# Remainders of three gate units formed by adding DMA transfers instead of subtractions on the vector engine

## The reference, cut to what matters

```python
h = rms_norm(x, attn_norm_g[l])
proj = jnp.matmul(h, w_in[l])            # 1024 x 4608
u_conv, q, k, v = ...                    # the first 2560 columns
gates = jax.nn.sigmoid(proj[..., o3:]).reshape(B, S, N_BRANCH, D)   # 2048 columns
conv_out = conformer_conv(u_conv, ...)   # depthwise, 31 taps, then layer norm and silu
...
merged = (gates[:, :, 0] * jnp.matmul(conv_out, w_conv_out[l])
          + gates[:, :, 1] * jnp.matmul(attn_out, w_attn_out[l]))
```

## Time and profile before

| | |
|---|---|
| median of 2 runs | 1041.17 us (1039.8 to 1042.54) |
| profiled execution | 1040.6 us, span 1038.8 us |
| busy: PE, DVE, ACT, POOL | 906.6, 458.1, 350.5, 8.0 us |
| mean granted TensorE clock | 0.941 |
| read from HBM | 298.84 MB, 289 GB/s over the span |

### The profile page before, as it was taken

The page is one execution under the profiler, slowest core; times in us unless marked ns, Lnnn a source line. Parts: engine busy times, 40 slices in busy tenths (PEclk is TensorE's granted clock), DMA queues, the critical chain, the costliest instruction groups (busy, mean ns, idle before and its releaser), DMA issues.

```text
span 1038.8 us, 14337 instructions
## 1 busy us (share of the span) xinstructions
PE 906.6 (87%) x6040; PEld 659.7 (64%) x6040; DVE 458.1 (44%) x804; ACT 350.5 (34%) x561; POOL 8.0 (1%) x14
## 2 busy tenths in 40 slices
PE   8999999999889947858775766999999989999997
PEld 7969878955246411313222131488999989999886
DVE  6899858511010010100101010188656676988752
ACT  5453483311010000100000010349565645756542
POOL 1000000000000000000000000000100000000000
PEclk9999999999999987978888896999999999999999
DMA  9866434989999999999999999982524245664451
GB/s 332 295 224 228 178 122 170 393 338 420 415 411 426 382 429 423 426 425 425 429 418 432 421 428 425 404 290 82 166 101 160 86 158 163 198 206 166 168 197 41
DMA packets 78493, 301.27 MB, mean 290 GB/s; under 512 B 4195, under 2 KB 30948, under 8 KB 62818
## 3 DMA queue, kind: packets, MB, share of 16 engines
q1 hardware_dynamic: 76640, 298.82, 73.0%
q10 hardware_dynamic: 1458, 1.07, 0.4%
q0 software_dynamic: 336, 0.53, 0.3%
HBM read 298.84 MB, written 1.05 MB: 289 GB/s over the span
## 4 chain that ended last, share of the span: by engine, by line
PE 59%; DMA 27%; DVE 8%; ACT 3%; issue 1%; SPq 1%; DVEq 0%; ACTq 0%
PE bank L1412 11%; DMA ring<-in_w_gate_e_dram 9%; DMA ring<-in_w_down_e_dram 8%; PE bank L1079 8%; DMA ring<-in_w_up_e_dram 7%; PE bank L1430 6%; PE bank L1303 3%; PE bank L1318 3%; PE bank L781 3%; PE bank L1137 3%; PE bank L688 2%; PE bank L715 2%; DVE big L1971 2%; DMA qvpr<-in_w_down_e_dram 2%; PE bank L1109 2%; PE bank L955 2%
## 5 line engine op out<-in xcount | busy, mean ns | idle before, releaser
L1079 PE MATMUL bank<-ring,big 128*32 128x512 f32 x768 | 163.9, 711 | 76.5 <-DMA ring<-in_w_up_e_dram 38.6
L1079 PEld LDWEIGHTS bank<-ring,big 128*32 128x32 f32 x768 | 38.8, 127 | 193.8 <-issue 90.1
L352 DVE TENSOR_TENSOR ring_parts<-ring,ring_parts 128x2048 fp32r<-128x2048 f32 (+1 forms) x54 | 118.8, 2248 | 35.9 <-ACT ring_parts L344 35.5
L344 ACT ACTIVATE ring_parts<-ring 128x2048 fp32r<-128x2048 f32 (+1 forms) x53 | 96.6, 1874 | 55.5 <-DMA ring<-in_w_up_dram 26.1
L2261 DVE TENSOR_TENSOR xT<-bank,xT 128x512 f32<-128x512 f32 x32 | 22.1, 692 | 137.0 <-PE bank L1123 137.0
L1412 PE MATMUL bank<-mrg_parts,ring_parts 128*128 128x256 f32 x640 | 82.3, 281 | 0.0
L1412 PEld LDWEIGHTS bank<-mrg_parts,ring_parts 128*128 128x128 f32 x640 | 78.5, 189 | 0.0
L2218 DVE TENSOR_TENSOR big<-big,const 128x128 f32<-128x128 f32 x14 | 3.5, 289 | 154.4 <-PE bank L1066 154.4
L1079 PE MATMUL bank<-hs,big 128*32 128x512 f32 x128 | 67.8, 683 | 0.0
L1109 PE MATMUL bank<-ring,big 128*32 128x512 f32 x336 | 45.8, 673 | 18.9 <-DMA ring<-in_w_down_e_dram 16.8
L1079 PE MATMUL bank<-qvpr,big 128*32 128x512 f32 x112 | 60.7, 696 | 0.6 <-DMA qvpr<-in_w_gate_e_dram 0.6
(11 more groups left out here) (423 smaller groups left out, 1627.3 us busy)
## 6 DMA issues: line engine op xcount, KB each, us to landing
ring<-in_w_up_e_dram SPq DMA_DIRECT2D x24, 2048.0 KB, 28.8
ring<-in_w_gate_e_dram SPq DMA_DIRECT2D x24, 2048.0 KB, 22.4
ring<-in_w_down_e_dram SPq DMA_DIRECT2D x17, 2048.0 KB, 21.5
ring<-in_w_in_dram SPq DMA_DIRECT2D x12, 2048.0 KB, 14.2
ring<-in_w_up_dram SPq DMA_DIRECT2D x22, 1024.0 KB, 7.2
ring<-in_w_down_e_dram SPq DMA_DIRECT2D x12, 1024.0 KB, 20.3
ring<-in_w_down_dram SPq DMA_DIRECT2D x5, 2048.0 KB, 7.9
ring<-in_w_out_dram SPq DMA_DIRECT2D x4, 2048.0 KB, 9.8
```

Source lines behind the costliest of these rows:

```text
L344: signal(act.activation(pairs[stage][u % 3][0][:, part], raws[stage][u % 3][:, part], ACT.Copy), stage + "_hi")
L352: signal(eng.tensor_tensor(lo[:, part], raws[stage][u % 3][:, part], hi[:, part].bitcast(F32), ALU.subtract), name)
L1079: mm = pe.matmul(bank[part][CAP * j:CAP * j + CAP, :], xeT[:, c, CAP * j:CAP * j + CAP], w[j][c], start=(c == 0), stop=(c == DC - 1))
```

## The change

For gate units 0, 1 and 2 the remainder is no longer formed by DVE. ACT writes the rounded weights with their sign turned (`scale=-1.0`) into `GATE_HI`, and then copies that, -hi, over the weights in their slot. GpSimd's queue then reads the same weights from HBM a second time with DMAs that add to what is in the slot (`accum_op=ALU.add`): -hi + W = lo. It issues two such DMAs of 1 MB for a unit, one for each half, and waits for both of a unit before it issues those of the next. PE multiplies (-hi) x h1_hi, (-hi) x h1_lo, and, now as the third product, lo x (-h1_hi), so that the whole sum has its sign turned; the sigmoid takes that back with `scale=-1.0`. The negated activations `h1_neg` are two further copies of 1024 columns on ACT. The semaphore `gate_hi` now counts four steps for a unit, `gate_lo` 16 for each DMA.

```diff
+        h1_neg = [parts["mrg"][:, T * k:][:, 0:T] for k in range(4)] + [parts["sq"][:, T * k:][:, 0:T] for k in range(4)]
...
             signal(pool.tensor_copy(pairs["in"][0][0][:, h:], raws["in"][0][:, h:]), "in_hi")
+            for u in range(3):
+                if u:
+                    pool.wait_ge(S["gate_lo"], 32 * u)
+                for i in range(2):
+                    pool.wait_ge(S["gate_hi"], 4 * u + 2 + i + 1)
+                    dst = ring_r[PLAIN_AT[1 + u]][:, 2048 * i:2048 * i + 2048].rearrange("p (k n) -> p k n", k=4)
+                    pool.dma_start(dst, w_plain[1 + u][:, 4 * i:4 * i + 4].bitcast(F32R), accum_op=ALU.add).then_inc(S["gate_lo"], 16)
...
-                            if m == 0 and k % 4 == 0 and which < 2:
-                                pe.wait_ge(S[("gate_hi", "gate_lo")[which]], 2 * u + k // 4 + 1)
-                            w = lo[:, k] if which == 1 else hi[k // 4][:, k % 4]
-                            x = h1_lo[:, k * T:k * T + T] if which == 2 else h1_hi[k]
+                            if m == 0 and k % 4 == 0 and which == 0:
+                                pe.wait_ge(S["gate_hi"], 4 * u + k // 4 + 1)
+                            if (m, which, k) == (0, 2, 0):
+                                pe.wait_ge(S["gate_lo"], 32 * (u + 1))
+                                pe.wait_ge(S["h1_hi"], 6)
+                            w = lo[:, k] if which == 2 else hi[k // 4][:, k % 4]
+                            x = (h1_hi[k], h1_lo[:, k * T:k * T + T], h1_neg[k])[which]
...
-                move(("gt", m), big[:, m * T:m * T + T], T, ACT.Sigmoid)
+                move(("gt", m), big[:, m * T:m * T + T], T, ACT.Sigmoid, scale=-1.0 if m < 12 else 1.0)
...
                 for i in range(2):
-                    signal(act.activation(GATE_HI[u][i], ring[PLAIN_AT[1 + u]][:, 2048 * i:2048 * i + 2048], ACT.Copy), "gate_hi")
+                    signal(act.activation(GATE_HI[u][i], ring[PLAIN_AT[1 + u]][:, 2048 * i:2048 * i + 2048], ACT.Copy, scale=-1.0),
+                           "gate_hi")
+                for i in range(2):
+                    act.wait_ge(S["gate_hi"], 4 * u + i + 1)
+                    signal(act.activation(ring_r[PLAIN_AT[1 + u]][:, 2048 * i:2048 * i + 2048], GATE_HI[u][i].bitcast(F32), ACT.Copy),
+                           "gate_hi")
             arrive(act, ("k", 3))
             round_gates(0)
+            for m in range(4):
+                copied(act, ("ca", m))
+            signal(act.activation(parts["mrg"][:, 0:1024], parts["qko"][:, 2048:3072].bitcast(F32), ACT.Copy, scale=-1.0), "h1_hi")
             round_gates(1)
             for t in range(TT):
                 move(("v", t), vtok[:, 512 * t:512 * t + 512], 512)
             b = arrive(act, ("qn", 0))
             emptied(act.activation(q_root, b[:, 0:16], ACT.Sqrt, bias=EPS, scale=1.0 / 64), ("qn", 0))
+            signal(act.activation(parts["sq"][:, 0:1024], parts["mrg"][:, 1024:2048].bitcast(F32), ACT.Copy, scale=-1.0), "h1_hi")
...
-            def rest_of_gates(u):
-
-                for i in range(2):
-                    dve.wait_ge(S["gate_hi"], 2 * u + i + 1)
-                    part = slice(2048 * i, 2048 * i + 2048)
-                    signal(dve.tensor_tensor(ring_r[PLAIN_AT[1 + u]][:, part], ring[PLAIN_AT[1 + u]][:, part],
-                                             GATE_HI[u][i].bitcast(F32), ALU.subtract), "gate_lo")
-
-            rest_of_gates(0)
-            rest_of_gates(1)
             queries_and_keys()
-            rest_of_gates(2)
             convolve((2, 3), first_maxima)
```

## The result

The changed kernel takes 1057.76 us (median of 2 runs, 1056.09 to 1059.44) against 1041.17 before: a ratio of 1.0166 with a 95% interval of 1.0147 to 1.0185, slower by 16.6 us, which is less than 2%. Five more runs of the same kernel later gave 1055.75 us against 1040.21, or 1.015 (1.0135 to 1.0165), 15.5 us. The profiled execution took 1059.4 us, with a span of 1057.6.

What follows compares the result with a forecast made beforehand. It took TensorE, with 0.2 us of slack, and DVE as level limits; PE waits of 3.2, 3.9 and 10 us, 17.1 together, less 0.2, added to 1040.6 gave 1057.5 us, in a range of 1041 to 1080.

Steps and rivals of the forecast that it cites:

- ACT and DVE: Before the mean: DVE loses 4.5 us of subtraction, ACT's load delays its reciprocals 4.0; at most 0.2 us gained.
- the second negation: ACT work that unit 0's third product needs, ending at 78.0: PE waits at least 1.3 us even with free transfers.
- The price of a unit: Two 1 MB adds per gate unit: 3.0 us fixed plus 10.9 us moving, 13.9 us.
- The doubled reading: Gate units' adds read old and new words, two passes at the loads' rate: 10.9 us a unit instead of 5.4.
- Unit 1's wait: PE at unit 1's third product: landing at 95.2, wanted at 91.3, so a wait of 3.9 us.
- the meeting with SyncE's loads: End of unit 1's adds: SyncE's two 2 MB loads, issued at 89.6, meet the last 1.3 us, moving landing to 95.2.
- Unit 2's wait: PE at unit 2's third product, adds beside the loads: 0.7 to 11.6 us, taken as 10 us.
- GpSimd's 64 KB transfer: Earlier copy landing after 6.3 us beside a load; taken as sign for unit 2's wait near the upper end, 10 us.
- The later stages: Stages after 120 us: all shifted by one constant, found again at 1038 us.
- Hidden adds: Rival for the gate units: one pass, 8.4 us a unit, landing before PE asks; 1041.7 us, chance 0.20.
- GpSimd's own pace: Rival for the gate units: adds at GpSimd's queue rate, 22.7 us a unit; 1072 us, up to 1085, chance 0.27.
- DVE's relief: Rival before the mean: DVE arrives early because ACT is quicker; capped at PE's 0.2 us, no separate chance given.

Runs made afterwards that it cites:

- Experiment 1: Changed kernel without its six adding transfers, remainder left out, PE waiting for ACT's copies instead: 1041.15 us, 1.0006 of the kernel before.
- experiment 7: Kernel before, with only unit 2's remainder formed by adds and two more ACT passes: 1039.95 us, 0.9995.
- experiment 2: Changed kernel with its six adding transfers made plain copies from the same queue: 1041.22 us, 1.0008 of the kernel before.
- experiment 8: Changed kernel with 6 and 20 spare float32 matmuls before PE's waits in units 0 and 2: 1056.05 us, 1.0154 of the kernel before.
- experiment 3: Changed kernel with SyncE's loads for the next stage held until unit 2's adds have landed: 1045.32 us, 1.0051 of the kernel before.
- Experiments 4: Changed kernel with 11 and 36 spare float32 matmuls before PE's waits in units 0 and 2: 1060.42 us, 1.0193 of the kernel before.
- 10: Changed kernel with 20 spare float32 matmuls before PE's wait in unit 2 alone: 1054.70 us, 1.014 of the kernel before.
- experiment 9: Changed kernel run again as it is, as a control: 1055.75 us, 1.015 of the kernel before.
- experiment 5: Changed kernel with a semaphore for each unit, GpSimd not waiting for landings between units: 1044.23 us, 1.0044 of the kernel before.
- experiment 6: Changed kernel with own semaphores, ACT writing negatives in place, no negated activations, other loads issued after unit 2's adds: 1041.57 us, 1.0017 of the kernel before.

## Why the prediction was right, and where it was not

The forecast was 1057.5 us and the measurement 1057.76; rows of the trace, not the total, say how far the reasons were right.

**ACT and DVE** held as worked out. Experiment 1 shows the 1.2 us of the second negation (expected at least 1.3). In experiment 7 DVE's 4.5 us go from the chain, and the kernel is 1.5 us faster to 0.4 us slower, the interval of its ratio; its chain is PE's alone, so behind DVE stood a level PE, as the prediction said.

**The price of a unit** held: a fixed 3.0 and a moved 10.9, 13.9 us, stand against 13.7 from landing to landing (79.87 to 93.59), and 80.0 against 79.87 for unit 0. Its two parts were each off by some 0.7 us, and against each other: at the measured 207 GB/s, 2.1 MB move in 10.1 us, which leaves 3.6 for the fixed part. The doubled reading behind it agrees with experiment 2, where the same bytes move at 382 to 403 GB/s without the addition and at 207 with it. The Trainium skill (Collectives: The Full Stack, "The bandwidth ceiling: the fold count and why AG ≠ RS ≠ AR") has the rule that the prediction drew on, both operands read through one ring at half the rate, for the reduce step of a collective. The adds of this one core come close to it, a factor of 1.85 to 1.95; no trace here shows the two reads themselves.

**Unit 1's wait** was too large: 0.6 us, where 3.9 stood. Two parts failed. PE came 1.8 us later than worked out because of the clock, so it wanted the unit at 93.1 and not at 91.3. And the landing was 93.6, not 95.2, chiefly because the 1.3 us for the meeting with SyncE's loads did not arise. That the loads went out at 91.2 and not at 89.6 explains little of it: in experiment 8 they did go out at 89.62, and unit 1 landed 13.9 us behind unit 0, against 13.7 here and 13.7 in experiment 3, where no loads ran. The term measures 0.2 us.

**Unit 2's wait** was 9.6 us for a forecast of 10, but the reason given was partly wrong. The prediction took a value near the upper end because GpSimd's 64 KB transfer of the earlier trace rows looked worse than equal turns. That the queues take turns packet by packet, as the Trainium skill says (DMA: Bandwidth & Descriptors, "Queues, rings and completion order"), the trace agrees with: 581 packets to 671. As the adds' packets take longer, they had more than half of the engines' time. The value came out right because PE, too, wanted the unit 1.4 us earlier than forecast (107.05 for 108.4), and the unit landed at 116.6 for 118.4. The late 64 KB row should not have been carried over to a queue with megabytes in it.

**The missing term** is the granted clock behind a wait: 1.8 us after unit 0's and 2.4 after unit 2's (11.94 less 9.49), nowhere in the sum. The waits were 17.1 us in the sum and 13.0 on the chip; the 4.2 us of the clock stand almost exactly in the gap. The total was right because two errors met, and that is luck. Experiments 4, 8 and 10 tie the slow matmuls to the idle time: with PE kept at work they run at a clock of 1.00. They also show that such time comes back only where the next wait doesn't take it, and the control of experiment 9 shows it from the other side: no fall of the clock at unit 0, a wait of 2.0 us instead of 0.6 at unit 1, and the mean at nearly the same time. The 1.8 us at unit 0 are therefore no loss of their own as long as unit 1 lands when it does.

**The later stages** shifted by about one constant, as predicted: PE at matching places lags by 17.1 us at 169, 16.1 at 220 and 16.3 at 666. Some 1.5 us are given back between the mean and 220 us. At the mean itself it is 0.5, since the kernel before spent 2.34 us there (114.22 to 116.56), with its waits for DVE, and the changed one 1.89. From there to 213 us the lag stays at 17.1. Then the changed kernel gains another 1.25 between its 214.2 and 219.0 us, and for that the profiled execution of the kernel *before* is the reason: there its granted clock fell.

```profile
198.00:200.00 2.00, 2.00 (x13) 2.00 (x12) 1.52 (x11) 1.57 (x3) 0.00 (x0) 0.60 0.91 381
200.00:202.00 2.00, 2.00 (x9) 1.79 (x8) 1.91 (x18) 2.00 (x3) 0.00 (x0) 0.55 0.52 218
```

In the changed kernel the same work ran at 1.00, as it did in experiment 9. So this part is no effect of the change. The profiled execution of the changed kernel ends 18.8 us later. Near 735 us it shows 7.14 us for matmuls that take 5.48 before, in a fall of the clock there (0.66 from 735 to 740). Two single executions can thus differ by 1 to 2 us at one place by the clock alone; in the medians the difference is 16.6.

**The rivals.** Hidden adds (1041.7) failed for the changed kernel, but not because the adds are too slow for the empty stretch from 68.8 to 86.4: two of three units would have come in time if GpSimd had not waited between them (experiment 5). The prediction named that wait and never asked what the sum would be without it. GpSimd's own pace (1072) failed: 13.7 us a unit, not 22.7. DVE's relief was worth nothing.

The prediction called 2% about what a measurement of this kernel can tell. The interval of the ratio is 0.2% to either side, so 1.6% is a clear loss.

**What stays open:** when a wait of 2 to 3 us lowers the clock and when it doesn't, how the clock's part in the whole kernel stands outside its noise, and what an add does inside the DMA engines that takes the 1.85 to 1.95 times of a copy.

## What to carry to other kernels

Before work is moved to a queue that waits for its own transfers, lay the landings end to end as a chain of their own, beside the plain loads that will start by then: here the waits between the units, which needed only separate semaphores, cost more than the slowness of the adds themselves (1055.75 us with them, 1044.23 without, 1040 before). Two level engines mean that freeing one of them is worth the other's slack and no more. And a wait put into a busy TensorE can cost more than its length in its own stretch, through the clock: not behind the waits up to 2.0 us here, mostly behind those of 2.3 to 2.9, and both times behind those of 9.4 and more. Where another wait stands behind it, that one takes the difference.

## What the runs showed of the hardware

- A transfer from HBM that adds into SBUF moved 207 GB/s with all DMA engines full; the same transfer as a plain copy, from the same queue, 382 to 403 (experiment 2).
- The issue of one 1 MB add held GpSimd for 1.26 to 1.83 us, that of a 1 MB copy for 0.74 to 0.91.
- From the issue of the first add to the first moved data passed about 2 us in experiment 6 (63.47 to 65.6), and about 3.5 to the full rate.
- Beside hardware loads the adding queue got nearly equal packets (581 to 671) and, since its packets take longer, 62.6% of the engines' time to the loads' 44.0%.
- The granted clock fell to 0.50 (1.2 GHz) with 2.86 us of idle TensorE as well as with 9.55 us, and the matmuls behind took 1.8 and 2.4 us more. It also fell with 2.68 us (experiment 5), 2.89 (3), 2.29 (8) and 2.74 (10), but not with 2.64 and 2.00 in experiment 9, nor with the 1.2 to 1.4 of experiments 1, 2 and 6. With a filling that left 0.81 us idle before unit 2 (10) it stayed at 1.00.
- The clock can fall in one execution and not in another of the same work: in the kernel before at 198 to 202 us (0.60 and 0.55).
- A float32 matmul of 256 columns has two records in the trace and takes 0.43 us, not the 0.23 that the section on the kernel before gives for line 688: that is the distance of the records. A matmul on the rounded format has one record and takes 0.12 us, so the three products of a split (0.36 us) are quicker than the one plain product.
